# Attention weights: from a product with a diagonal matrix to scaled rows and a plain transposition

## The reference

```
p = exp(s - max(s));  p = p / sum(p)          # masked softmax over the keys of the branch
o_branch = p @ v
o = g[0] * o_c + g[1] * o_s + g[2] * o_w       # sparse group: three branches, gates g per query and head
o = head_rms_norm(o) * silu(gate)
```

## Time and profile before

| | us |
|---|---|
| median of 3 runs | 2858.39 |
| lowest, highest | 2856.0, 4329.05 |
| the profiled execution, its own time | 2856.57 |
| its span in the trace | 2854.8 |
| attention stage in the span | 744 to about 989 |
| TensorE busy in the span | 2563.5 (90%) |
| DVE, ACT, POOL busy | 765.0, 536.5, 583.2 |

### The profile page before, as it was taken

How to read it: one execution, slowest core, us unless ns; L and a number is a source line. 1 busy time by engine, 2 the same in 40 slices (tenths; PEclk the granted TensorE clock), 3 DMA queues, 4 the chain that set the end, 5 groups by cost and what they waited for, 6 DMA issues and landing times. The chain is left out here.

```text
span 2854.8 us, 42314 instructions
## 1 busy us (share of the span) xinstructions
PE 2563.5 (90%) x18624; PEld 1660.1 (58%) x18624; DVE 765.0 (27%) x1528; ACT 536.5 (19%) x1076; POOL 583.2 (20%) x366
## 2 busy tenths in 40 slices
PE   4899977888799997999998978999999999999991
PEld 4788856677576743788875554445445445445440
DVE  2311015564355424223222342111111111111114
ACT  2011123442455312111110220000000100010001
POOL 2433323331111012422330002111111111111103
PEclk9999979998799998999999988999999999899995
DMA  3122221002110022211114017999999999999974
GB/s 154 67 96 89 89 79 40 20 16 76 61 60 1 1 81 81 60 53 36 59 45 195 34 66 283 403 394 394 401 400 395 402 404 389 397 404 392 395 327 189
DMA packets 86031, 537.39 MB, mean 188 GB/s; under 512 B 13336, under 2 KB 13592, under 8 KB 43472
## 3 DMA queue, kind: packets, MB, share of 16 engines
q1 hardware_dynamic: 69104, 498.60, 44.0%
q10 hardware_dynamic: 6496, 19.19, 1.9%
q0 software_dynamic: 10240, 16.82, 1.6%
HBM read 503.08 MB, written 43.52 MB: 191 GB/s over the span
## 5 line engine op out<-in xcount | busy, mean ns | idle before, releaser
L219 PE MATMUL banks<-arena 64*64 64x64 f32 (+11 forms) x15392 | 1873.0, 365 | 147.8 <-ACT arena L229 21.3
L219 PEld LDWEIGHTS banks<-arena 64*64 64x64 f32 (+3 forms) x15392 | 1085.2, 167 | 879.3 <-issue 735.1
L229 ACT ACTIVATE arena<-banks 128x512 f32<-128x512 f32 (+6 forms) x381 | 219.9, 587 | 1230.2 <-PE banks L219 595.8
L2602 POOL DMA_INDIRECT yb<-arena x64 | 65.1, 1018 | 913.0 <-DVE arena L2706 913.0
L224 PE MATMUL banks<-r,w2s 128*128 128x512 f32 x448 | 177.3, 396 | 19.1 <-POOL w2s L1983 19.1
L224 PE MATMUL banks<-r,wlo 128*128 128x512 f32 x432 | 171.1, 396 | 7.2 <-POOL wlo L414 7.2
L2715 DVE COPY arena<-banks 128x512 f32<-128x512 f32 x64 | 44.3, 692 | 490.8 <-PE banks L219 490.8
L225 PE MATMUL banks<-r,w2s 128*128 128x512 f32 x448 | 175.5, 392 | 0.0
L226 PE MATMUL banks<-r,w2s 128*128 128x512 f32 x448 | 175.1, 391 | 0.0
L226 PE MATMUL banks<-r,wlo 128*128 128x512 f32 x432 | 170.0, 394 | 0.0
L225 PE MATMUL banks<-r,wlo 128*128 128x512 f32 x432 | 169.6, 393 | 0.0
(11 more groups left out here) (240 smaller groups left out, 1571.0 us busy)
## 6 DMA issues: line engine op xcount, KB each, us to landing
arena<-in_wg SPq DMA_DIRECT2D x64, 2048.0 KB, 10.4
arena<-in_wu SPq DMA_DIRECT2D x64, 2048.0 KB, 14.9
arena<-in_wd SPq DMA_DIRECT2D x64, 2048.0 KB, 19.0
arena<-in_w SPq DMA_DIRECT2D x55, 512.0 KB, 3.3
spill<-arena SPq DMA_DIRECT2D x27, 512.0 KB, 2.6
arena<-spill SPq DMA_DIRECT2D x27, 512.0 KB, 6.0
arena<-yb SPq DMA_DIRECT2D x8, 1024.0 KB, 12.7
arena<-in_x SPq DMA_DIRECT2D x12, 512.0 KB, 5.2
```

The costliest lines, as they stand in the source:

```text
L219: return pe.e.matmul(o, l, r, start=start, stop=stop)
L229: return act.e.activation(o, i, ACT.Copy)
L2602: return pool.e.indirect_dma_start(yb, bass.IndirectOffsetOnAxis(ap=six[:, col:col + 1].bitcast(U32), axis=0), src[:, :], None, bounds_che ...
```

## The change

The factors are no longer carried by a diagonal matrix. The four rows of a unit (2 heads x 2 query blocks) are multiplied in place in `Pb` by their factor: three by DVE, directly behind the factors in its queue (`dve_scale_rows`), and one, head 1 with the first query block, by POOL (`pool_scale_rows`). TensorE turns the scaled block by a transposition, with the identity as the other operand, and waits for both engines' semaphores. `Dg` and `pool_diagonal` are gone.

```diff
-    Dg = [sb(f"Dg{i}", [128, 4, 128], c=c3_) for i in range(3)]
...
-    def pool_diagonal(pool, u):
-
+    def scaled_row(u, h, jj):
+        br = UNITS[u][2]
+        return Pb[br][:, h, jj, 0:n_keys(br, 2 * UNITS[u][0] + jj)], scl[:, u % 4, 2 * h + jj:2 * h + jj + 1]
+
+    def dve_scale_rows(dve, u):
+        dve.wait_ge(s("scaled"), u + 1)
+        for h, jj in ((0, 0), (0, 1), (1, 1)):
+            p, f = scaled_row(u, h, jj)
+            t = dve.e.tensor_scalar(p, p, f, None, ALU.mult)
+        t.then_inc(s("rows_scaled").sem, 1)
+
+    def pool_scale_rows(pool, u):
         pool.wait_ge(s("scaled"), u + 1)
-        if u >= 3:
-            w = ps["turn", u - 3, keys_blocks(u - 3)[-1]]
-            pool.wait_ge(w.full, w.v)
-        pool.e.tensor_tensor(Dg[u % 3][:, :, :], bc4(ident), scl[:, u % 4, :].unsqueeze(2).to_broadcast([128, 4, 128]),
-                             ALU.mult).then_inc(s("diagonal").sem, 1)
+        p, f = scaled_row(u, 1, 0)
+        pool.e.tensor_scalar(p, p, f, None, ALU.mult).then_inc(s("rows_scaled_pool").sem, 1)
...
-        pe.wait_ge(s("diagonal"), u + 1)
+        pe.wait_ge(s("rows_scaled"), u + 1)
+        pe.wait_ge(s("rows_scaled_pool"), u + 1)
...
-                t = mm(pe, b.t[0:n, c * 128:(c + 1) * 128], Pb[br][:, h, j_, at:at + n], Dg[u % 3][:, c, :], True, True)
+                t = pe.e.transpose(b.t[0:n, c * 128:(c + 1) * 128], Pb[br][:, h, j_, at:at + n], ident)
...
                 dve_scale(dve, v - 1)
+                dve_scale_rows(dve, v - 1)
...
-                pool_diagonal(pool, v - 1)
+                pool_scale_rows(pool, v - 1)
```

## The result

The changed kernel takes 2877.82 us (median of 5 runs, 2874.66 to 2880.55) against 2858.39 before. The ratio is 1.007, 95% interval 1.0054 to 1.0086: some 20 us slower. By the 2% bound that is "within 2%", but the sign and the time of the forecast (2835, range 2816 to 2862) were wrong. The profiled execution took 2880.26 us for a span of 2878.3. One of the five runs before took 4329.05 us; no trace explains it, and the median does not depend on it.

The account below looks back on a forecast made before the run. TensorE was taken to bound the attention stage; gains of 5 (J=0), 6.5 (J=1), 9.3 (J=2, J=3) and 2 us (last units) made 23 off 2856.57, and with 1.8 for the median 2835 us, range 2816 to 2862.

Parts of the forecast that it names:

- Point 1: TensorE's turning in the attention stage: one 110 ns transposition replaces two records a block, ceiling 42 us.
- Points 2 and 4: POOL's 32 row scalings take 35 us, as before; beside DVE, an 896-wide row lands 3.9 us after its factors.
- DVE undisturbed: When POOL and DVE scale rows together, DVE keeps its speed and POOL ends 0.45 us later per wide DVE scaling.
- Point 3: DVE's 96 new row scalings add at most 44 us in the stage, fitting as throughput.
- point 6: In J=2 and J=3, waits for exponentials and ACT's copies swallow gain, leaving 9.3 us; DVE's waiting hides rows elsewhere.
- points 5 to 7: Attention stage: late rows and window maxima, gain swallowed by waits, and the sum over quarters, together 23 us.
- Point 7: Sum over the attention stage's quarters and last two units: 23 us gained, bounds 0 and 42.
- Rival C: TensorE's clock drops from 800 to 980 us as its busy share falls: 2876 us, chance 0.07; in full 2950, 0.02.
- Rival A: The whole turning gain arrives, POOL's rows not stretched: 40 us less, 2818 us, chance 0.14.
- D: Transpositions on TensorE take half of 110 ns: 60 us less, 2798 us, chance 0.01.
- B: DVE scalings are held while POOL works, adding POOL's 35 us to DVE's rows: 2852 or 2862 us, chance 0.18.

Follow-up runs that it names:

- Experiment 3: The change with all four rows of a unit scaled on DVE and none on POOL: 2876.59 us, ratio 1.0069.
- Experiment 4: The change with DVE's three rows behind the gating and mean square instead of ahead of them: 2860.76 us, ratio 1.0018.
- experiments 2 and 8: The change, blocks turned by a product with the identity: 2889.25 us; the change with rows behind gating and mean square, each transposition issued twice: 2867.58 us.
- experiment 1: The change without any scaling of rows, that part of the computation left out, transpositions only: 2842.27 us, ratio 0.9941.
- experiment 10: The change plus eight unused transpositions ahead of TensorE's wait for each unit's rows: 2868.58 us, ratio 1.0036.
- experiments 4 to 6: The change with DVE's rows behind gating and mean square, 2860.76 us; at the turn's end, 2862.94; there with all four on DVE, 2862.01.
- experiment 11: All rows scaled by DVE at the turn's end, but all 16 units of J=2 and J=3 keep POOL's diagonal and product: 2860.92 us, ratio 1.0012.
- experiment 12: Eight unused transpositions before each row wait, in the kernel keeping diagonals for selected and window units of J=2 and J=3: 2862.57 us, ratio 1.0013.
- experiment 9: All rows scaled by DVE at the turn's end, but selected and window units of J=2 and J=3 keep POOL's diagonal and product: 2854.78 us, ratio 0.9992.

## Why the prediction was wrong

- **Point 1 held.** 360 records for 720, about 114 ns at full clock (110 forecast). The saved work was there; it did not arrive.
- **Points 2 and 4, POOL's wide row, held.** The 896-wide row ends 3.49 us after its start (3.9 forecast after the factors), TensorE waits 2.1 us (2.3). The sum did not: POOL's busy time rose by 11 us (583.2 to 594.1), where point 2 had the rows take as much as the diagonals. **DVE undisturbed failed**: the second row takes about twice as long, 1501 ns for 746. Experiment 3 shows that all this costs nothing net.
- **Point 3's size held**: DVE has 42 us more busy time, at most 44 forecast.
- **The step that failed is the last sentence of point 6**: "The cover that hides the DVE rows elsewhere is DVE's own waiting for TensorE." On it points 5 to 7 costed DVE's rows at nothing outside one place, the window unit's maxima. DVE's waits are spare time of the engine, but not at the moment at which the rows stand in its queue: behind the factors come gating and mean square, and the bank of the latter is one of TensorE's two for turning: 12.5 us of TensorE's waits, where the forecast has none. The order of calls, told ahead of the prediction, has it, and the prediction never asked who waits for them. Experiment 4, with only that order changed, brings back 15 of the 20 us; experiments 2 and 8 put the order at 22 us (32 less 10) where TensorE's work is as before.
- **Point 7's gain, 23 us net of the rows, was too large** even with no rows (experiment 1: 17). The mechanism of point 6, exponentials and copies, was right and under-counted: 14 us more of TensorE's waits in the whole stage in experiment 1.
- **The sum of the two traced executions** shows where the 40 us went. In the stage TensorE's waits grew from 26 to 64 us, 38 more. Its busy time fell by 15 in place of 40, so 25 us went into work at the low clock. Less 40, plus 38, plus 25 is 23 us, and the spans differ by 23.5. The forecast had about 17 us of new waits (40 less 23) and nothing for the clock.
- **Rival C, the clock, got 0.07, and raising it by filler gave back half of the loss.** TensorE's busy share from 860 to 979 us fell to 74% (88.27 of 119) and the clock to 0.86. The 2876 us of C is close to the 2878 measured, but not by its own mechanism alone: C knew nothing of the mean square, and experiment 4 keeps a clock of 0.87 at 5 us over before. That the clock is a cause and not only a sign is shown by experiment 10: about 10 us, with 256 transpositions of work added. The argument from the earlier trace rows is weaker than it reads: there 1.2 GHz is inferred from the doubled durations alone, while the clock column of the same stretches (30 to 46 us) reads 1.00. The 15 us of the order and the 10 us of the clock are not added up: shorter waits in experiment 4 are also fewer reasons for the clock to fall, though it fell all the same.
- **Rival A** fell with experiment 1: more than half of the ceiling is gone before any row is scaled. **D** fell with the 114 ns of a transposition. **B** was right that DVE slows beside POOL and wrong that this decides.
- **The noise was put too high.** The forecast took 2% (57 us) for what a measurement can tell from no change; the interval here is 0.3% wide, and a loss of 20 us stands clear of it.

What stays open: how the 25 us of the low clock and the longer waits share the 20 us, since a wait can lower the clock and a slower clock can hide a wait; how the remaining 5 us over before in experiments 4 to 6 split between the two; and why rows in J=0 and J=1 bring no gain at all (experiment 11), which a higher clock alone did not mend (experiment 12, in the kernel of experiment 9).

## What to carry to other kernels

Idle time of an engine hides added work only if nothing that someone waits for stands behind it in the queue at that moment: for each inserted instruction, list what follows it down to the engine's next wait, and for each of these who needs its buffer, scratch uses of a shared ring included. An engine that bounds a stage and is made quicker leaves gaps, and on TensorE the gaps can be paid twice, as here, where the granted clock fell from 1.00 to 0.86. If it falls, first shorten the waits, and value saved work at far less than its duration (here 40 us of work were worth 5 to 17 us). Where the moved work comes in several widths, try it for the narrow ones alone, as experiment 9 did.

## What the runs showed of the hardware

- A scaling of 128x1024 f32 in SBUF on DVE takes 749 ns alone. Beside one scaling on POOL the second of DVE's three rows takes 1501 ns and the third 742, 1121 on average. At 512 columns both are slowed, 809 and 743 ns for 481. POOL's own row of 896 columns takes 3488 ns in place of 2.5 us, the estimate that the earlier trace rows give without company.
- Beside an addition of 2.35 us on POOL one DVE scaling of 512 columns took 2562 ns in place of 481.
- TensorE's clock fell to 1.2 GHz behind waits of 2.09 and 1.73 us with 1.6 us of work between them, and did not where the first was 0.66 us behind filler (granted clock 0.50 and 1.00).
- Doubling 360 transpositions raised the clock from 860 to 979 us from 0.87 to 0.99 and cost 5 us for 40 us of work, and 256 useless ones made a kernel 10 us faster.
